# Seven block products with their sums taken in PSUM by later matmuls, in place of sums on VectorE

## The chip, the cores and the metric

One core of a Trainium2 chip runs the whole program. The time is that of the device, in microseconds (us). Before: 1896.96 us, the median of three executions (1893.1 to 1897.03). A difference below 0.2% (3.8 us) can't be told from none.

## The reference, cut to what matters

Two layers of a diffusion backbone over 384 tokens (128 of a prompt, 256 of a sample), all in fp32. Each layer projects the normalised tokens h, runs three attention mixers with 16 jobs in all (8 latent heads "mla", 4 grouped-query jobs "gqa", 4 differential heads "diff"), weighs the three outputs with sigmoid gates and ends in 16 experts:

```
z = h @ p['w_in']                      # among its columns g_mla, g_gqa, g_diff, and dq, dk, dv
merged = (sigmoid(g_mla) * (o_mla @ w_br_mla) + sigmoid(g_gqa) * (o_gqa @ w_br_gqa)
          + sigmoid(g_diff) * (o_diff @ w_br_diff))
x = x + gate1 * (merged @ w_out)       # then norm, router, top-k, experts, residual
```

The gate columns, and dq, dk, dv for the sample's tokens, are matrix products of a 2x2 block form. The kernel computes each by seven block products instead of eight (the scheme of Strassen and Winograd), with A and B cut in four:

```
M1 = a11 b11   M2 = a12 b21   M5 = s1 t1   M6 = s2 t2   M7 = s3 t3   M3 = s4 b22   M4 = a22 t4
C11 = M1 + M2          C12 = (M1 + M6) + M5 + M3
C21 = (M1 + M6) + M7 + M4          C22 = (M1 + M6) + M7 + M5
```

C11 and C12 are the halves of `first`, C21 and C22 those of `second` (C21 is columns 0 to 191 of it).

## The kernel before, in words

Every engine has its program written out by hand, with semaphores between them. TensorE is the engine that is always busy; work of VectorE, ScalarE and GpSimd is laid beside it.

**The jobs.** A layer's attention runs as jobs i = 0 to 15. For job i TensorE issues `scores(i)`, `prep(i+1)` (transposes of the next queries and keys), `values(i-1)` (the product "pv" of the job before, only behind odd jobs for mla), then the list `FILL[i]`, which keeps it busy while the softmax runs, and `turn_probs(i)`. ScalarE runs in the order prep(i+1), the exponentials of job i (`exps`, L999), the copy of pv(i-1) out of PSUM (`values`, L1022, L1026, L1030), then its part of FILL[i]. VectorE runs maxima, prep(i+1) (L1343 to L1350), `normalise` (L1361, L1370, L1365), then its part of FILL[i]. Each engine takes its own list strictly in order.

**The blocks.** A block is seven products ("gate" of branch b and unit u, or "two" of half f and q), each of four matmuls with 192 columns; the trace has eight records for each product. They are issued in `product` (L1989) and `two` (L2013). Blocks stand in FILL[5], [6], [7] (gate 0), FILL[8], [9] (two blocks each, behind two projections "c2" of L1951, which ScalarE copies out in L1043), FILL[12] to [15] (gate 1, then two "br1" products of L2041, and in 13 to 15 one "square"), and, behind the jobs, four blocks of gate 2: its first product FILL[16] comes before pv(15), the others are in LAST_GATES. That is 15 blocks in a layer, 30 in all. FILL[7] also has ("adat", 2): two transposes, whose result VectorE takes in L1280.

**The sums.** Before, the order of a block is M5, M1, M2, M6, M3, M7, M4, each product in a bank of its own. ScalarE copies M5 and M1 into PM5 and PM1 (L1053). VectorE does seven additions: L1415 (M2 + PM1), L1417 and L1418 (M6 + PM1 into PU2, + PM5 into PM1), L1421 (M3), L1423 and L1424 (M7), L1426 (M4). Then ScalarE takes the tanh of the pair (L1057). The tanh lets VectorE do the branch's L1393 and L1395.

**The banks.** PSUM has 8 banks. The scores use 0 to 3. `user_banks` gives every product, pv, c2, branch and square ("user") a bank: of 4 to 7, or of 6 and 7 alone for the last two of a fill and outside fills, the one whose last use is oldest. `BEFORE` names the user that held the bank last, and `user_bank` (L1787) makes TensorE wait until ScalarE or VectorE has read that one. Banks 4 and 5 are lent by prep and turn_probs (`borrow`, L2049). Behind the last gate block VectorE copies WB2 (L1572), for which the matmuls of L2325 wait.

Of the kernel before, what the change touches and what calls it, by code (L numbers as in the profile page):

```python
# [18 lines left out]
ALU = mybir.AluOpType  # L19
# [123 lines left out]
M5, M1, M2, M6, M3, M7, M4 = PRODUCTS  # L143
# [5 lines left out]
FILL[7].insert(2, ("adat", 2))  # L149
# [8 lines left out]
FILL[NJ].append(("gate", 2, 0, M5))  # L158
# [45 lines left out]
def by_dve(user):  # L204

    return user[0] in BY_DVE or user[0] in ("gate", "two") and user[3] not in (M5, M1)
# [17 lines left out]

def user_banks():
# [12 lines left out]
    return bank, before  # L238
# [5 lines left out]
BLOCKS = [u for u in USERS if u[0] in ("gate", "two") and u[3] == M5]  # L244


def block_before(user):

    n = BLOCKS.index(user[:3] + (M5,))
    return BLOCKS[n - 1][:3] if n else None  # L250

# [171 lines left out]
DVE_LINKS = 139  # L423
# [3 lines left out]
def backbone(nc, a):  # L427
    ctx = ExitStack()
    with ctx:
# [155 lines left out]

        def held(g, e, c):

            first = c * GE * CAP + e * CAP
            return XG[:, first:first + XW]
# [71 lines left out]
        def _(sp):  # L661
# [8 lines left out]
                     11: [(rows_out, 32), (user_dve, evacuated(USER_AT["gate", 2, 3, M4]))], 12: merged, 13: merged,  # L670
                     14: [(user_mm, USER_AT["out", 0, 1] + 1)], 15: gated, 16: normed,
                     17: jobs_done + [(user_dve, evacuated(USER_AT["gate", 2, 3, M4]))]}
# [50 lines left out]
        def _(pool):  # L723
# [93 lines left out]
            for l in range(DEPTH):  # L817
# [61 lines left out]
                pool.wait_ge(user_dve.s, user_dve.at(l, evacuated(USER_AT["two", 1, 1, M4])))  # L879
# [49 lines left out]
        def _(act):  # L929
# [106 lines left out]
            def fill(l, key):  # L1036
# [9 lines left out]
                elif kind in ("gate", "two"):  # L1046
                    b, u, m = key[1:]
                    if m in (M5, M1):
                        before = block_before(key)
                        if before:  # L1050
                            free = USER_AT[before + ((M7,) if m == M5 else (M3,))]
                            act.wait_ge(user_dve.s, user_dve.at(l, evacuated(free)))
                        user(l, key, lambda ps: nc.scalar.copy(PM5 if m == M5 else PM1, ps[:, 0:HALF]))  # L1053
                    if kind == "gate" and m == M4:
                        pair = (MG[:, 2 * u:2 * u + 2], SG1, SG2[:, 2 * u:2 * u + 2])[b]
                        act.wait_ge(user_dve.s, user_dve.at(l, evacuated(USER_AT[key])))
# [150 lines left out]
        def _(dve):  # L1207
# [190 lines left out]
            def product(l, key):  # L1398


                b, u, m = key[1:]
                n = USER_AT[key]
                if m in (M5, M1):
                    return
                dve.wait_ge(user_mm.s, user_mm.at(l, n + 1))
                ps = PS[:, BANK[n], 0:HALF]
                if key[0] == "two":
                    c = 768 * b + TOK * u
                    first, second = ZD[:, 1, c:c + TOK], ZD[:, 2, c:c + TOK]
                else:  # L1410
                    first, second = ((MG[:, 2 * u], MG[:, 2 * u + 1]), (SG1[:, 0], SG1[:, 1]),
                                     (SG2[:, 2 * u], SG2[:, 2 * u + 1]))[b]
                if m == M2:
                    dve.wait_ge(user_act.s, user_act.at(l, evacuated(USER_AT[key[0], b, u, M1])))
                    ins = nc.vector.tensor_tensor(first[:, 0:HALF], ps, PM1, ALU.add)  # L1415
                elif m == M6:
                    link(nc.vector.tensor_tensor(PU2, ps, PM1, ALU.add), l)  # L1417
                    ins = nc.vector.tensor_tensor(PM1, PU2, PM5, ALU.add)  # L1418
                elif m == M3:
                    dve.wait_ge(user_dve.s, user_dve.at(l, evacuated(USER_AT[key[0], b, u, M6])))  # L1420
                    ins = nc.vector.tensor_tensor(first[:, HALF:TOK], ps, PM1, ALU.add)  # L1421
                elif m == M7:
                    link(nc.vector.tensor_tensor(PU2, ps, PU2, ALU.add), l)  # L1423
                    ins = nc.vector.tensor_tensor(second[:, HALF:TOK], PU2, PM5, ALU.add)  # L1424
                else:
                    ins = nc.vector.tensor_tensor(second[:, 0:HALF], ps, PU2, ALU.add)  # L1426
                ins.then_inc(user_dve.s, 1)
# [51 lines left out]
            for l in range(DEPTH):  # L1479
# [40 lines left out]
                for i in range(NJ + 1):  # L1520
# [17 lines left out]
                    for key in FILL[i]:  # L1538
                        if key[0] in ("gate", "two"):
                            product(l, key)  # L1540
                            if i in (14, 15) and key[3] == M4:
# [18 lines left out]
                for key in LAST_GATES:  # L1560
# [4 lines left out]
                    if key[2:] == (0, M4):  # L1565
                        inverse(l, 3).then_inc(recd_ok.s, 1)
                    if key[2:] == (1, M4):
# [203 lines left out]
        def _(pe):  # L1771
# [203 lines left out]
            def product(l, key):  # L1975
# [12 lines left out]
                for k in range(4):  # L1988
                    ins = pe.matmul(ps[:, 0:HALF], lhs[:, k], rhs[:, k], start=k == 0, stop=k == 3)  # L1989
# [6 lines left out]
            def two(l, key):  # L1996
# [14 lines left out]
                done = {M1: units[0:2], M3: units[2:4]}.get(m) if q else None  # L2011
                for k in range(4):
                    ins = pe.matmul(ps[:, 0:HALF], lhs[:, k], rhs[k], start=k == 0, stop=k == 3)  # L2013
# [543 lines left out]
```

## Time and profile before

| | us |
|---|---|
| median of three executions | 1896.96 |
| the profiled execution, its own time | 1892.48 |
| its span, first to last instruction | 1890.7 |
| TensorE busy | 1758.8 (93% of the span) |
| VectorE busy | 672.1 (36%) |
| ScalarE busy | 332.8 (18%) |
| GpSimd busy | 320.1 (17%) |

The mean granted TensorE clock is 0.987 of full speed. The jobs with blocks of the first layer lie at 157 to 375 us, its last gates at 375 to 416, its experts at 513 to 945. The second layer repeats this 935.7 us later. In the rows PE is TensorE, DVE VectorE, ACT ScalarE, POOL GpSimd. A row of a timeline gives the start, the length, and in square brackets how long the engine was idle before it and who ended that; x8 is eight instructions merged in one row.

### The profile page before, as it was taken

The numbers are of one execution on the slowest core, as the hardware profiler recorded it, in microseconds if no ns is written. First come the engines' busy times: TensorE is split into PE (matmuls) and PEld (weight loads), VectorE is DVE, ScalarE is ACT, GpSimd is POOL, SyncE is SP. The second block draws the span as 40 slices with busy tenths as digits, with TensorE's granted clock in tenths as the row PEclk, the third lists the DMA queues.
The fourth block names the chain that finished last, engine by engine and source line by source line (L and its number), as shares of the span: only waits on it lengthen the run. The fifth ranks groups of instructions, "written<-read, shape, count | busy, mean of one in ns | idle before, by whom it ended". The sixth has DMA issues, their size and how long they took to land.

```text
span 1890.7 us, 21687 instructions
## 1 busy us (share of the span) xinstructions
PE 1758.8 (93%) x8638; PEld 977.0 (52%) x8638; DVE 672.1 (36%) x1385; ACT 332.8 (18%) x818; POOL 320.1 (17%) x349
## 2 busy tenths in 40 slices
PE   7999999999999998889799999999998999897886
PEld 5557877784533323233255587788844333332322
DVE  2235547742412212121123554567423221211212
ACT  3332213220201001000032322232112010100101
POOL 0234654320000000000002446523200000000000
PEclk9999999999899999999999999999999999999999
DMA  9245231249499999999961632322548999999997
GB/s 372 107 180 218 95 119 49 88 184 418 180 429 429 429 429 429 429 430 428 427 236 53 270 146 79 123 79 101 225 191 349 430 428 429 429 428 430 429 428 296
DMA packets 58227, 541.15 MB, mean 286 GB/s; under 512 B 7001, under 2 KB 7433, under 8 KB 14353
## 3 DMA queue, kind: packets, MB, share of 16 engines
q1 hardware_dynamic: 56592, 535.65, 68.5%
q0 software_dynamic: 1536, 4.13, 0.6%
q8 instruction: 70, 1.15, 0.2%
q14 instruction: 29, 0.23, 0.0%
HBM read 536.54 MB, written 3.21 MB: 285 GB/s over the span
## 4 chain that ended last, share of the span: by engine, by line
PE 78%; DMA 12%; DVE 4%; SPq 3%; ACT 2%; issue 1%; DVEq 0%; ACTq 0%
PE banks L2437 25%; PE banks L1989 10%; DMA arena<-in_w_exp 7%; PE banks L1951 7%; PE banks L2041 7%; PE banks L1798 4%; PE banks L2356 4%; PE banks L2013 4%; SPq L695 3%; DMA ring<-in_w_exp 3%; PE banks L2516 2%; PE banks L1906 2%; PE banks L2214 2%; PE banks L2155 1%; PE banks L2412 1%; DMA ring<-in_w_att 1%
## 5 line engine op out<-in xcount | busy, mean ns | idle before, releaser
L2437 PE MATMUL banks<-arena 128*64 128x512 f32 x1680 | 382.1, 599 | 28.8 <-DMA arena<-in_w_exp 17.0
L2437 PE MATMUL banks<-ring,arena 128*64 128x512 f32 x1392 | 313.0, 595 | 23.4 <-DMA ring<-in_w_exp 13.3
L2437 PEld LDWEIGHTS banks<-arena 128*64 128x64 f32 x1680 | 117.5, 138 | 271.8 <-issue 220.0
L2437 PEld LDWEIGHTS banks<-ring,arena 128*64 128x64 f32 x1392 | 97.0, 137 | 222.0 <-issue 178.0
L1734 DVE TENSOR_TENSOR arena<-banks,arena 32x512 f32<-32x512 f32 (+1 forms) x128 | 87.9, 687 | 265.7 <-PE banks L2437 264.4
L1951 PE MATMUL banks<-ring,arena 128*128 128x384 f32 (+1 forms) x416 | 132.8, 478 | 0.7 <-ACT arena L949 0.7
L1798 PE MATMUL banks<-arena 128*128 128x128 f32 (+3 forms) x734 | 107.9, 283 | 26.5 <-DVE arena L1719 18.9
L1798 PEld LDWEIGHTS banks<-arena 128*128 128x128 f32 (+3 forms) x734 | 84.2, 142 | 87.6 <-issue 37.6
L2041 PE MATMUL banks<-arena,ring 128*128 128x384 f32 x384 | 126.8, 488 | 0.0
L1189 ACT ACTIVATE arena<-banks 128x512 f32<-128x512 f32 x32 | 19.1, 597 | 508.5 <-PE banks L2437 508.5
L1951 PEld LDWEIGHTS banks<-ring,arena 128*128 128x128 f32 x416 | 78.2, 190 | 50.9 <-issue 1.5
L823 POOL COPY arena<-arena 128x32 f32<-128x32 f32 x4 | 0.8, 210 | 598.2 <-ACT arena L1087 597.9
L1989 PE MATMUL banks<-ring 128*128 128x192 f32 x544 | 96.9, 328 | 0.8 <-DVE arena L1395 0.8
L2041 PEld LDWEIGHTS banks<-arena,ring 128*128 128x128 f32 x384 | 72.2, 190 | 48.8 <-issue 1.5
L1719 DVE TENSOR_TENSOR arena<-arena,banks 128x512 f32<-128x512 f32 x32 | 22.0, 687 | 209.4 <-PE banks L2437 209.4
L1989 PEld LDWEIGHTS banks<-ring 128*128 128x128 f32 x544 | 89.0, 190 | 2.8 <-DVE arena L1395 1.3
L2356 PE MATMUL banks<-ring,arena 128*128 128x512 f32 x192 | 86.4, 604 | 1.2 <-DVE arena L1395 1.2
L1716 DVE TENSOR_TENSOR arena<-banks,arena 128x512 f32<-128x512 f32 x32 | 22.1, 691 | 171.4 <-ACT arena L1189 171.4
L925 POOL TENSOR_TENSOR arena<-arena 128x1024 f32<-128x1024 f32 x1 | 2.4, 2363 | 442.6 <-DVE arena L1744 442.6
L999 ACT ACTIVATE arena<-banks,arena 128x384 f32<-128x384 f32 x144 | 71.4, 508 | 19.0 <-DVE arena L1335 18.7
L2516 PE MATMUL banks<-arena 128*128 128x512 f32 (+1 forms) x112 | 51.9, 617 | 21.7 <-DVE arena L1734 18.6
L1333 DVE TENSOR_REDUCE arena<-banks 128x1 f32<-128x384 f32 x144 | 58.4, 460 | 28.0 <-PE banks L2155 16.5
(264 smaller groups left out, 2110.8 us busy)
## 6 DMA issues: line engine op xcount, KB each, us to landing
arena<-in_w_exp SPq DMA_DIRECT2D x69, 2048.0 KB, 30.7
ring<-in_w_exp SPq DMA_DIRECT2D x69, 2048.0 KB, 29.6
ring<-in_w_att SPq DMA_DIRECT2D x80, 1024.0 KB, 7.0
arena<-in_w_exp SPq DMA_DIRECT2D x72, 1024.0 KB, 26.7
ring<-in_w_exp SPq DMA_DIRECT2D x36, 1024.0 KB, 13.4
ring<-in_w_att SPq DMA_DIRECT2D x26, 768.0 KB, 7.9
arena<-in_w_att SPq DMA_DIRECT2D x12, 1024.0 KB, 11.6
ring<-in_w_att SPq DMA_DIRECT2D x8, 672.0 KB, 8.7
```

The source lines that it names most:

```text
L695: sp.dma_start(span(group), a["w_exp"][l, c0:c1].rearrange("(p n) -> p n", p=P))\
L999: ins = nc.scalar.activation(PB[:, b, lo:hi], PS[:, 2 * m + bank, c:c + hi - lo], ACT.Exp, scale=SCALE[kind], bias=NB[:, b, r:r + 1], accu ...
L1333: ins = nc.vector.reduce_max(MX[:, b, r:r + 1], PS[:, 2 * m + bank, c:c + w], AX)
L1734: ins = nc.vector.tensor_tensor(y[32 * e:32 * e + hi - lo, BF * h:BF * h + BF], PS[64 * h + lo:64 * h + hi, 5], G2[64 * h + lo:64 * h + hi ...
L1798: return pe.transpose(out, src, IDT[0:rows, 0:rows])
L1951: ins = pe.matmul(ps[:, 0:width], hT[:, k, P * t:P * t + P], slots[n][:, c0:c0 + width], start=k == 0, stop=k == KC - 1)
L1989: ins = pe.matmul(ps[:, 0:HALF], lhs[:, k], rhs[:, k], start=k == 0, stop=k == 3)
L2013: ins = pe.matmul(ps[:, 0:HALF], lhs[:, k], rhs[k], start=k == 0, stop=k == 3)
L2041: ins = pe.matmul(ps[:, 0:TOK], w[:, k, P * (c % 4):P * (c % 4) + P], o[:, k], start=k == 0, stop=k == 3)
L2356: ins = pe.matmul(ps, MG[:, k, P * t:P * t + P], slots[n][:, c0:c0 + BF], start=k == 0, stop=k == KC - 1)
L2437: ins = pe.matmul(PS[64 * h:64 * h + 64, bank], lhs(k), slots[i][:, c0:c0 + BF], start=k == 0, stop=k == KC - 1)
L2516: ins = pe.matmul(combine_bank(g, n)[:, c:c1], w, YS[0 if t else 1][:, BF * h + c:BF * h + c1], start=True, stop=True)
```

## The change

The order of a block becomes M1, M5, M6, M2, M7, M3, M4. M6, M7 and M4 are added by TensorE to the bank in which M1 stands (start=False), and M3 to the bank of M5. Only M1, M5 and M2 open a bank. ScalarE copies the bank out after M1 (PM1), M5 (PM5), M6 (now PU2 = M1 + M6) and M4 (straight into C21). VectorE keeps three additions: M2 + PM1, M7's bank + PM5, M3's bank + PU2. So M6 waits for the copy of M1, M7 for that of M6, M3 for that of M5, and M4 for VectorE's reading of M7's bank.

A block in a fill has the banks 6 (M1 and its sums) and 7 (M5) and M2 in 4 or 5; the first of two blocks in a fill has 4 and 5, and M2 in 6 or 7. Behind the jobs they alternate between 6, 7 and 0, 1, with M2 and the last square in 2 or 3. ("adat", 2) moves from the third place of FILL[7] to the first. Worked through, `user_banks` gives: adat bank 7, and M5 behind it bank 7; c2's second projection bank 4, and M1 behind it bank 4; pv(5), pv(11) to pv(15) bank 7, and M5 behind each of them bank 7; the square of FILL[15] bank 6, and M1 of gate 2 behind it bank 6.

```diff
-M5, M1, M2, M6, M3, M7, M4 = PRODUCTS
+M1, M5, M6, M2, M7, M3, M4 = PRODUCTS
+OPENS, CLOSES = (M1, M5, M2), (M2, M3, M4)
...
-FILL[7].insert(2, ("adat", 2))
+FILL[7].insert(0, ("adat", 2))
...
-FILL[NJ].append(("gate", 2, 0, M5))
+FILL[NJ].append(("gate", 2, 0, M1))
...
-    return user[0] in BY_DVE or user[0] in ("gate", "two") and user[3] not in (M5, M1)
+    return user[0] in BY_DVE or user[0] in ("gate", "two") and user[3] in (M2, M7, M3)
...
-    bank, before, latest, holder = [], [], {6: -2, 7: -1}, {}
+    bank, before, latest, holder = [], [], {6: -2, 7: -1, 2: -4, 3: -3}, {}
+    after = [u for u in BLOCKS if u not in fill_of]
...
-        b = min((4, 5, 6, 7) if left > 2 else (6, 7), key=lambda x: latest[x])
+        block = user[:3] + (M1,)
+        if block in BLOCKS:
+            if left:
+                behind = sum(u in BLOCKS for u in FILL[i][FILL[i].index(block) + 1:])
+                sums, rest = ((6, 7), (4, 5))[::1 if behind % 2 == 0 else -1]
+            else:
+                sums, rest = ((6, 7), (0, 1))[after.index(block) % 2], (2, 3)
+            if user[3] == M2:
+                b = min(rest, key=lambda x: latest[x])
+            else:
+                b = sums[user[3] in (M5, M3)]
+        elif user[0] == "square" and not left:
+            b = min((2, 3), key=lambda x: latest[x])
+        else:
+            b = min((4, 5, 6, 7) if left > 2 else (6, 7), key=lambda x: latest[x])
...
-                elif kind in ("gate", "two"):
+                elif kind in ("gate", "two") and not by_dve(key):
                     b, u, m = key[1:]
-                    if m in (M5, M1):
+                    if m == M4:
+                        user(l, key, lambda ps: nc.scalar.copy(halves(key)[1][:, 0:HALF], ps[:, 0:HALF]))
+                    else:
                         before = block_before(key)
                         if before:
-                            free = USER_AT[before + ((M7,) if m == M5 else (M3,))]
+                            free = USER_AT[before + ({M1: M2, M5: M7, M6: M3}[m],)]
                             act.wait_ge(user_dve.s, user_dve.at(l, evacuated(free)))
-                        user(l, key, lambda ps: nc.scalar.copy(PM5 if m == M5 else PM1, ps[:, 0:HALF]))
+                        kept = {M1: PM1, M5: PM5, M6: PU2}[m]
+                        user(l, key, lambda ps: nc.scalar.copy(kept, ps[:, 0:HALF]))
...
-                if m == M2:
-                    dve.wait_ge(user_act.s, user_act.at(l, evacuated(USER_AT[key[0], b, u, M1])))
-                    ins = nc.vector.tensor_tensor(first[:, 0:HALF], ps, PM1, ALU.add)
-                elif m == M6:
-                    link(nc.vector.tensor_tensor(PU2, ps, PM1, ALU.add), l)
-                    ins = nc.vector.tensor_tensor(PM1, PU2, PM5, ALU.add)
-                elif m == M3:
-                    dve.wait_ge(user_dve.s, user_dve.at(l, evacuated(USER_AT[key[0], b, u, M6])))
-                    ins = nc.vector.tensor_tensor(first[:, HALF:TOK], ps, PM1, ALU.add)
-                elif m == M7:
-                    link(nc.vector.tensor_tensor(PU2, ps, PU2, ALU.add), l)
-                    ins = nc.vector.tensor_tensor(second[:, HALF:TOK], PU2, PM5, ALU.add)
-                else:
-                    ins = nc.vector.tensor_tensor(second[:, 0:HALF], ps, PU2, ALU.add)
-                ins.then_inc(user_dve.s, 1)
+                first, second = halves(key)
+                out, kept, of = {M2: (first[:, 0:HALF], PM1, M1), M7: (second[:, HALF:TOK], PM5, M5),
+                                 M3: (first[:, HALF:TOK], PU2, M6)}[m]
+                dve.wait_ge(user_act.s, user_act.at(l, evacuated(USER_AT[key[:3] + (of,)])))
+                nc.vector.tensor_tensor(out, ps, kept, ALU.add).then_inc(user_dve.s, 1)
...
-                    ins = pe.matmul(ps[:, 0:HALF], lhs[:, k], rhs[:, k], start=k == 0, stop=k == 3)
+                    ins = pe.matmul(ps[:, 0:HALF], lhs[:, k], rhs[:, k], start=k == 0 and m in OPENS, stop=k == 3 and m in CLOSES,
+                                    skip_group_check=True)
```

Left out: the same edit of the matmul in `two`, waits on M4's addition that now name M3's or M4's copy, `inverse` (L1455) that moves from behind M4 to behind M3, and the release of c2's weights, which moves from M1 to M6.

## Rows read from the trace of the kernel before

**Rows 1.** Busy time by stretch: us, then busy us (instructions) of each engine, clock, DMA.
```profile
157.00:416.00 259.00, 256.62 (x1456) 212.88 (x1454) 153.80 (x324) 70.64 (x201) 116.95 (x111) 1.00 0.28 105
1093.00:1352.00 259.00, 256.61 (x1455) 213.14 (x1454) 152.82 (x322) 70.77 (x201) 116.14 (x109) 1.00 0.28 105
513.00:945.00 432.00, 385.83 (x1776) 139.69 (x1774) 87.90 (x147) 30.19 (x62) 0.00 (x0) 0.98 1.01 429
480.00:513.00 33.00, 30.06 (x144) 19.21 (x144) 18.94 (x61) 10.15 (x22) 0.00 (x0) 0.79 0.40 162
```
**Rows 2.** Line 1053 alone: shortest, median and longest duration in ns.
```profile
L1053 ACT COPY arena<-banks x60: 299/318/366, 159.7 to 1344.2; 128x192 f32<-128x192 f32 x60
```
**Rows 3.** Timeline of job 5, a bank that TensorE waits for.
```profile
158.54 0.69 DVE L1344 COPY arena<-banks 64x512 f32<-64x512 f32 x1
...
159.29 0.43 PE L1989 MATMUL banks<-arena,ring 128*128 128x192 f32 x1 [0.18 <-DVE arena L1344]
```
**Rows 4.** Timeline of job 7, first layer.
```profile
184.02 1.47 PE L1989 MATMUL banks<-ring 128*128 128x192 f32 x8
...
185.32 1.46 PE L1989 MATMUL banks<-arena,ring 128*128 128x192 f32 x8
...
187.63 0.44 PE L1798 MATMUL banks<-arena 128*128 128x128 f32 x2 [0.84 <-DVE arena L1350]
...
187.90 1.47 PE L1989 MATMUL banks<-arena,ring 128*128 128x192 f32 x8
188.79 0.24 DVE L1280 TENSOR_TENSOR arena<-banks,arena 128x8 f32<-128x8 f32 x2
```
**Rows 5.** Timelines of jobs 12, 13, 15 and the last gates: second product, pv's copy.
```profile
302.13 1.46 PE L1989 MATMUL banks<-arena,ring 128*128 128x192 f32 x8
...
302.60 0.50 ACT L1026 COPY arena<-banks 128x384 f32<-128x384 f32 x1
...
321.30 2.12 PE L1989 MATMUL banks<-arena,ring 128*128 128x192 f32 x12
...
322.14 0.50 ACT L1030 COPY arena<-banks 128x384 f32<-128x384 f32 x1
...
360.22 2.60 PE L1989 MATMUL banks<-arena,ring 128*128 128x192 f32 x15
...
361.78 0.50 ACT L1030 COPY arena<-banks 128x384 f32<-128x384 f32 x1
...
378.08 1.46 PE L1989 MATMUL banks<-arena,ring 128*128 128x192 f32 x8
378.28 0.48 ACT L1030 COPY arena<-banks 128x384 f32<-128x384 f32 x1 [1.15 <-PE banks L2214]
```
**Rows 6.** Timeline of job 8: the first product behind the c2 projections.
```profile
209.54 1.46 PE L2013 MATMUL banks<-ring 128*128 128x192 f32 x8
209.74 0.48 ACT L1043 COPY arena<-banks 128x384 f32<-128x384 f32 x1 [4.68 <-PE banks L1951]
```
**Rows 7.** Timeline at the end of job 15.
```profile
373.97 1.13 DVE L1395 TENSOR_TENSOR arena<-arena 128x384 f32<-128x384 f32 x1
...
375.02 0.54 DVE L1449 TENSOR_SCALAR arena<-banks 128x384 f32<-128x384 f32 x1
375.15 1.57 PE L1989 MATMUL banks<-ring 128*128 128x192 f32 x8 [0.40 <-DVE arena L1395]
```
**Rows 8.** Timeline behind the last gate block.
```profile
415.38 0.61 PE L2325 MATMUL banks<-arena 2*128 2x16 f32 x4 [0.52 <-DVE arena L1572]
```
**Rows 9.** Busy time by stretch around a long and a shorter idle time of TensorE.
```profile
612.00:615.60 3.60, 0.50 (x5) 0.03 (x1) 2.76 (x4) 0.00 (x0) 0.00 (x0) 1.00 1.01 432
615.60:619.00 3.40, 3.40 (x6) 2.10 (x7) 0.69 (x1) 0.00 (x0) 0.00 (x0) 0.50 0.98 419
...
1372.00:1375.40 3.40, 2.16 (x6) 0.87 (x5) 1.49 (x3) 0.00 (x0) 0.00 (x0) 1.00 1.02 431
```
**Rows 10.** TensorE's waits behind VectorE: us in total, times, longest us.
```profile
PE banks L2516 <- DVE arena L1734: 18.6, 6, 3.1
```

More of the change, by code:

```diff
@@ L222, in evacuated @@
     return sum(by_dve(u) == dve for u in USERS[:n + 1])
+BLOCKS = [u for u in USERS if u[0] in ("gate", "two") and u[3] == M1]
 def user_banks():
     fill_of = {u: (i, len(FILL[i]) - k) for i in range(NJ) for k, u in enumerate(FILL[i])}
-    bank, before, latest, holder = [], [], {6: -2, 7: -1}, {}
+    bank, before, latest, holder = [], [], {6: -2, 7: -1, 2: -4, 3: -3}, {}
+    after = [u for u in BLOCKS if u not in fill_of]
     for n, user in enumerate(USERS):
@@ L241 @@
 BANK, BEFORE = user_banks()
-BLOCKS = [u for u in USERS if u[0] in ("gate", "two") and u[3] == M5]
 def block_before(user):
-    n = BLOCKS.index(user[:3] + (M5,))
+    n = BLOCKS.index(user[:3] + (M1,))
     return BLOCKS[n - 1][:3] if n else None
@@ L420 @@
 RAW_DVE, PROMPT_DVE = (1, 3, 4), (2,) + tuple(range(5, 4 + KC))
-DVE_LINKS = 139
+DVE_LINKS = 109
 POOL_LINKS = 58
@@ L584, in span, with halves @@
             return at(first, 2 * SLOT)
+        def halves(key):
+            kind, b, u = key[:3]
+            if kind == "two":
+                c = 768 * b + TOK * u
+                return ZD[:, 1, c:c + TOK], ZD[:, 2, c:c + TOK]
+            return ((MG[:, 2 * u], MG[:, 2 * u + 1]), (SG1[:, 0], SG1[:, 1]), (SG2[:, 2 * u], SG2[:, 2 * u + 1]))[b]
         def held(g, e, c):
@@ L878, in _ @@
                 pool.wait_ge(user_act.s, user_act.at(l, evacuated(USER_AT["c2", 7])))
-                pool.wait_ge(user_dve.s, user_dve.at(l, evacuated(USER_AT["two", 1, 1, M4])))
+                pool.wait_ge(user_act.s, user_act.at(l, evacuated(USER_AT["two", 1, 1, M4])))
+                pool.wait_ge(user_dve.s, user_dve.at(l, evacuated(USER_AT["two", 1, 1, M3])))
                 for t in range(2):
@@ L1398, in product @@
             def product(l, key):
[L1401 removed]
+                m = key[3]
+                if not by_dve(key):
+                    return
                 n = USER_AT[key]
[L1403 to L1404 removed]
                 dve.wait_ge(user_mm.s, user_mm.at(l, n + 1))
                 ps = PS[:, BANK[n], 0:HALF]
[L1407 to L1427 removed]
+                first, second = halves(key)
[3 more added lines that the diff above has]
+                nc.vector.tensor_tensor(out, ps, kept, ALU.add).then_inc(user_dve.s, 1)
             def token_sums_first(l):
@@ L1540, in _ @@
                             product(l, key)
-                            if i in (14, 15) and key[3] == M4:
+                            if i in (14, 15) and key[3] == M3:
                                 inverse(l, i - 14)
@@ L1564, in _ @@
                     product(l, key)
-                    if key[2:] == (0, M4):
+                    if key[2:] == (0, M3):
                         inverse(l, 3).then_inc(recd_ok.s, 1)
-                    if key[2:] == (1, M4):
+                    if key[2:] == (1, M3):
                         dve.wait_ge(rootd_ok.s, rootd_ok.at(l, 1))
@@ L2010, in two @@
                             M4: (a22, t4)}[m]
-                done = {M1: units[0:2], M3: units[2:4]}.get(m) if q else None
+                done = {M6: units[0:2], M3: units[2:4]}.get(m) if q else None
                 for k in range(4):
-                    ins = pe.matmul(ps[:, 0:HALF], lhs[:, k], rhs[k], start=k == 0, stop=k == 3)
+                    ins = pe.matmul(ps[:, 0:HALF], lhs[:, k], rhs[k], start=k == 0 and m in OPENS, stop=k == 3 and m in CLOSES,
+                                    skip_group_check=True)
                     if k == 0:
```

7 lines of the change are left out of this document (4 added, 3 removed).

## The prediction, made before the changed kernel ran

> **What bounds the kernel now.** First the busy time by stretch. In the 259.0 us of the first layer that hold every block, TensorE is busy for 256.62, at full clock, and in the second layer for 256.61 [rows 1]. The reader is to see that 2.4 us a layer is all that TensorE idles there: no relief of VectorE can bring more than about 4.8 us in both layers together, while any new wait of TensorE is paid in full. Next VectorE in the same row. It is busy for 153.80 of the same 259 us, so it bounds nothing [rows 1]. Last the timelines, for two questions at each block: which user held the bank before, and when was it read? They are what decides here, since each engine takes its list in order.
>
> **Units of the working.** Products follow each other by 185.32 - 184.02 = 1.30 us [rows 4]. Where TensorE waits for a reader, the restart can be priced: L1344 ends at 158.54 + 0.69 = 159.23, the waiting matmul begins at 159.29 and is 0.10 longer than the normal 0.33 of a matmul with 192 columns [rows 3]. So work goes on **0.16 us after the end of the read**. And since a matmul's row reaches 0.16 beyond the start of the next (eight rows last 1.46, not 1.30), a printed idle time of x is a loss of x + 0.16.
>
> **What the change removes and adds.** Of VectorE's seven additions four go, 120 in all. ScalarE gets two more copies a block of 0.32 us [rows 2], 60 in all, about 19 us. TensorE has the same matmuls. Adding to a bank is what three of four matmuls in each product do already, in rows of the same length; I take nothing for it, and know of no row for a gain or a loss. The four additions and the copies are hidden behind TensorE. If the cover of the copies were gone, it would cost M6 and M7 up to 0.32 each.
>
> **Waits inside a block.** M6 adds to M1's bank, and one product (1.30 us) lies between. A copy starts about 0.4 us behind a product's last matmul, lasts 0.32 and is seen 0.16 later: 0.9 of the 1.46 us to the first matmul of M6. The same holds for M7 behind M6's copy and for M4 behind VectorE's addition. So they cost nothing while ScalarE is free. In the jobs it first does the exponentials and pv's copy. In job 12 that copy ends at 303.10 [rows 5]; M1's follows and frees M6 at about 303.6, while M6's turn, behind an M5 that starts at 303.26 (below), is 304.56. I count nothing more. A square root on ScalarE between two copies of gate (2, 1) is counted at nothing too; some tenths at most.
>
> **The banks across users** are where it costs. Per layer:
> - *pv and M5.* M5, now second, takes bank 7, which held the pv product issued just before the block. Its copy stands on ScalarE behind the exponentials. Before, the fourth or fifth product had that bank. Job 12: the second product starts at 302.13; the copy ends at 302.60 + 0.50, so M5 starts at 303.26: 1.13 us lost. Job 13: 322.14 + 0.50 + 0.16 = 322.80 against 321.30, 1.50; job 14 repeats it, 1.50. Job 15, with no prep before it: 362.44 against 360.22, 2.22. The last gates: 378.28 + 0.48 + 0.16 = 378.92 against 378.08, 0.84 [rows 5]. Job 6 has the same pattern with 0.28. Sum **7.47**.
> - *adat in job 7.* Moved to the front it takes bank 7, and M5 takes bank 7 behind it. VectorE reads adat only after its key copies and `normalise`: 188.79 + 0.24 [rows 4], so M5 starts at 189.19, with adat and M1 done and six products to go: end at 189.19 + 7.80 = 196.99. Before, five products were to go at 187.90 (a wait of 0.84 for L1350 included, which disappears): end at 194.40 [rows 4]. **2.59**.
> - *c2 and M1.* M1 takes bank 4, from which c2's second projection is just being copied: 209.74 + 0.48 + 0.16 = 210.38 against 209.54 [rows 6], 0.84. Jobs 8 and 9: **1.68**.
> - *The square.* M1 of the last gates waits for L1449 on bank 6, ending at 375.56, where it waited for L1395, ending at 375.10 [rows 7]: **0.46**.
> - *Gains.* The wait for L1344 goes, 0.18 + 0.16 + 0.10 = 0.44 with the restart [rows 3]; one for a slow L1418 in job 6, 0.2; and L1572 no longer stands behind an addition of the last product: 0.52 + 0.16 = 0.68 [rows 8]. **-1.32**.
>
> 7.47 + 2.59 + 1.68 + 0.46 - 1.32 = 10.88 us a layer, **21.8 us** in both; the second layer's rows repeat the first's. SP's queue keeps its transfers, and the waits it gets are not later ones. GpSimd's block sums are awaited by M5, now one product later.
>
> **TensorE's clock.** It stood at full speed in both stretches with the blocks [rows 1]. Job 7's new wait leaves TensorE idle for some 3.4 us at a time. An idle time of 3.10 us before 615.6 was followed by 3.4 us at half the clock, that is 1.2 GHz instead of 2.4, in which 1.7 us of work are lost; one of 1.24 us, within 1372.0 to 1375.4, was not [rows 9]. The trace has six idle times of 3.10 us, all for L1734 [rows 10]; by the clock column four were followed by such a spell. Bounds for the clock: nothing, or four spells (job 7 and job 15 in both layers), 6.8 us. I take the two of job 7, the rows nearest to them being those of 3.10: 3.4 us.
>
> Sum: 21.8 + 3.4 = **25.2 us**. The profiled execution has a span of 1890.7 and a time of 1892.48, so it would go to 1915.9 and 1917.7. It lies 4.5 us below the median of the executions shown, a difference between executions that no step of mine touches. Forecast: 1896.96 + 25.2 = **1922.1 us**.
>
> **Rivals.**
> 1. *The clock falls in every long wait.* By the Trainium skill ("TensorE: Matmul & The Clock Gate", section "A second HAM failure mode: psum-queue depth-cycling") short idle times between groups of matmuls that cycle through banks are enough to make the clock go down and up. The waits of jobs 7 and 12 to 15 would each bring a spell of 1.7 us: 10 x 1.7 = 17 us in place of 3.4, 1935.8 us. Against it: the idle time of 1.24 us [rows 9], as long as those of jobs 13 and 14 would be printed, left the clock up. Chance 0.07. By that rule the sum is 38.8 us, by the rows 25.2.
> 2. *The experts' transfers take the loss up.* From 513 to 945 the DMA engines move 429 GB/s all the time [rows 1]. If that stream kept its times, TensorE would come late to the experts and find the weights there. Against it: from 480 to 513 they move only 162 [rows 1], since all places are full until TensorE uses one, so the stream starts with TensorE and shifts with it. Wholly taken up, the time is 1897; by half, 1908 to 1910. Chance 0.08, half of it for no measurable difference.
> 3. *Faster: ScalarE comes in time.* With VectorE's queue shorter, maxima and exponentials could end sooner, so that pv's copy is over before the second product. The point at which this decides is in job 12: the copy has to end by 301.97 and not at 303.10 [rows 5], and in job 15 2.2 us earlier. Then adat has to be read early as well. What remains are the gains, 2 x 1.32 = 2.6 us, and at most the 4.8 us of idle time: 1892 to 1894. Against it: in those jobs the exponentials follow maxima that VectorE does before any of the additions that go. Chance 0.03.
> 4. *Fewer of the waits appear.* If pv's copies were awaited but M5's place were mostly covered, only adat, c2 and the square would be left: 2 x (4.73 - 1.32) = 6.8 us, 1903.8. Nothing in the profile says so. Chance 0.05.
>
> **How the numbers follow.** The forecast has 0.77. Its own range is 1916 to 1927: the sum without a clock spell is 1918.7, with four 1925.5, and executions differ by some us. The range for 8 in 10 goes down to 1909, to the case of half the loss taken up, and up to 1931, towards the clock. Within 0.2% (about what a measurement of this kernel can tell from no change): 0.04, from rival 2. Faster: 0.03. Slower: 0.93.
>
> **What would show it.** In the profile after: idle time of L1989 put down to ScalarE's L1026 and L1030 in jobs 12 to 15, 0.9 to 2.0 us each as printed; one of some 3.4 us in job 7, put down to VectorE's L1280; 0.6 us of L2013 behind ScalarE's L1043, four times; TensorE's busy time in the blocks' stretch unchanged but the stretch some 11 to 13 us longer; the experts' stretch as long as before. The prediction is wrong if TensorE's idle time before L1989 and L2013 together stays under 10 us in both layers, or if the experts' stretch gets shorter.

## The result: slower by 1.35%, and where the time went

| | before | after |
|---|---|---|
| median of five executions | 1894.88 us | 1918.68 us |
| the profiled execution, its span | 1890.7 us | 1919.6 us |

The ratio is 1.0135, with a 95% interval of 1.0122 to 1.0147: 23.1 to 27.9 us on 1894.88. The two medians differ by 23.8 us. The forecast was 1922.1 us, the range 1909 to 1931.

The trace has 8638 matmul records of TensorE in both kernels, in the same order but for the two transposes of adat in each layer, so the start of the n-th record of one can be subtracted from that of the other. That shift grows by 1.45 us ahead of the first block, by 13.57 us in the first layer's stretch with blocks, by 13.42 us in the second's, and by 0.43 us in all the rest, experts included: 28.9 us. The 27.0 us of the two stretches are the change; what lies ahead of the blocks differs from one execution to the next (in the kernels below the shift there is between -0.7 and +2.1 us). The profiled execution of after, at 1921.46 us, was the slowest of its five, which is one reason why 27.0 is more than the 23.8 us between the medians.

Busy time of the kernel after, by stretch, in the columns of [rows 1]:

```profile
157.00:427.00 270.00, 258.88 (x1434) 212.95 (x1433) 126.09 (x263) 79.27 (x229) 117.02 (x113) 0.99 0.27 100
1105.00:1375.00 270.00, 258.88 (x1433) 212.44 (x1432) 122.50 (x263) 79.52 (x230) 119.25 (x114) 0.99 0.27 100
525.00:957.00 432.00, 384.53 (x1788) 140.72 (x1789) 89.14 (x152) 32.11 (x67) 0.00 (x0) 0.99 1.01 429
```

Against [rows 1] TensorE now idles 11.1 us in each stretch with blocks instead of 2.4, and the clock is at 0.99 instead of 1.00. VectorE is busy for 126 us instead of 154, and TensorE got nothing of it. The idle time explains 8.7 of the 13.5 us of a stretch; most of the rest is the clock, of which more below, since matmuls at half speed count as busy. The experts' stretch keeps its 429 GB/s. Who is waited for (engine and line of the waiting instruction, engine and line that ended the wait, us in total, times, longest):

```profile
PE banks L2002 <- ACT arena L1055: 10.0, 8, 2.0
...
PE banks L2002 <- DVE arena L1309: 6.8, 2, 3.4
...
PE banks L2027 <- ACT arena L1068: 2.3, 4, 0.6
...
PE banks L2002 <- ACT arena L1051: 1.7, 2, 0.9
...
PE banks L2002 <- DVE arena L1462: 0.6, 2, 0.3
```

L2002 and L2027 are the block products (before: L1989, L2013). L1055 and L1051 are ScalarE's copies of pv, L1309 is VectorE's reading of adat, L1068 the copy of c2, L1462 the square's. Each of these is a bank's reader that was not awaited before: eighteen waits, 21.4 us as printed, plus a restart each.

The groups of the additions and copies (busy us, mean ns): three additions a block are left on VectorE, and ScalarE has four copies:

```profile
L1440 DVE TENSOR_TENSOR arena<-banks,arena 128x192 f32<-128x192 f32 x90 | 32.2, 358 | 198.2 <-PE banks L2002 121.0 <-PE banks L2027 77.3
...
L1081 ACT COPY arena<-banks 128x192 f32<-128x192 f32 x90 | 28.4, 318 | 83.3 <-PE banks L2002 56.4 <-PE banks L2027 26.7
...
L1074 ACT COPY arena<-banks 128x192 f32<-128x192 f32 x30 | 9.6, 320 | 144.1 <-PE banks L2002 105.5 <-PE banks L2027 38.6
```

Jobs 7 and 15 in the timeline of after, where [rows 4] and [rows 5] show the kernel before:

```profile
185.31 1.47 PE L2002 MATMUL banks<-arena,ring 128*128 128x192 f32 x8
...
190.15 4.55 PE L2002 MATMUL banks<-ring 128*128 128x192 f32 x16 [3.38 <-DVE arena L1309]
...
195.83 1.46 PE L2002 MATMUL banks<-ring 128*128 128x192 f32 x8
...
197.13 1.46 PE L2002 MATMUL banks<-arena 128*128 128x192 f32 x8
...
372.92 0.50 ACT L1055 COPY arena<-banks 128x384 f32<-128x384 f32 x1
...
373.47 4.20 PE L2002 MATMUL banks<-ring,arena 128*128 128x192 f32 x16 [1.96 <-ACT arena L1055]
```

The products at 195.83 and 197.13 are M7 and M3, added to banks that ScalarE has read: 1.30 us from one to the next, as in [rows 4]. But behind the two waits something is longer. Sixteen matmul records of two products should last 2.87 us behind a wait (that is what they last behind the 1.23 us in job 13). Here they last 4.55 and 4.20. The cause stands in the clock column of the windows:

```profile
190.50:193.90 3.40, 3.40 (x13) 3.40 (x12) 0.40 (x2) 0.32 (x1) 0.00 (x0) 0.50 0.00 0
374.80:378.20 3.40, 3.40 (x13) 3.40 (x12) 0.23 (x1) 0.64 (x2) 2.88 (x3) 0.51 0.00 0
```

TensorE's granted clock is half, 1.2 GHz instead of 2.4, for 3.4 us behind both waits. The second layer shows the same twice (from 1139.4 and 1323.7 us), which makes four spells in this execution. No trace shows how many the other four executions had.

### The profile page after: what moved, and what is told of

It reads as the page before. It is cut to its first block, busy times and chain, and to the rows that moved or that the text cites. A ratio compares the mean times of both kernels' runs of the same rounds, so it can differ in the third digit from the quotient of the medians.

```text
span 1919.6 us, 21699 instructions
## 1 busy us (share of the span) xinstructions
PE 1767.0 (92%) x8638; PEld 980.6 (51%) x8638; DVE 613.0 (32%) x1265; ACT 352.3 (18%) x878; POOL 317.7 (17%) x349
## 4 chain that ended last, share of the span: by engine, by line
PE 76%; DMA 12%; DVE 5%; ACT 3%; SPq 3%; issue 1%; DVEq 0%; ACTq 0%
PE banks L2452 25%; PE banks L2002 10%; DMA arena<-in_w_exp 7%; PE banks L1964 7%; PE banks L2056 7%; PE banks L2027 4%; PE banks L1811 4%; PE banks L2371 4%; SPq L719 3%; DMA ring<-in_w_exp 3%; PE banks L2531 2%; PE banks L1919 2%; PE banks L2170 1%; DMA ring<-in_w_att 1%; PE banks L2427 1%; PE banks L2297 1%
## 5 line engine op out<-in xcount | busy, mean ns | idle before, releaser
L2002 PE MATMUL banks<-ring 128*128 128x192 f32 x544 | 102.0, 335 | 12.1 <-DVE arena L1309 6.8
L2002 PEld LDWEIGHTS banks<-ring 128*128 128x128 f32 x544 | 92.7, 195 | 15.4 <-DVE arena L1309 7.3
L1440 DVE TENSOR_TENSOR arena<-banks,arena 128x192 f32<-128x192 f32 x90 | 32.2, 358 | 198.2 <-PE banks L2002 121.0
L1024 ACT ACTIVATE arena<-banks,arena 128x384 f32<-128x384 f32 x144 | 71.5, 509 | 18.3 <-DVE arena L1364 18.0
```

Of the source, the lines that this page charges most:

```text
L1024: ins = nc.scalar.activation(PB[:, b, lo:hi], PS[:, 2 * m + bank, c:c + hi - lo], ACT.Exp, scale=SCALE[kind], bias=NB[:, b, r:r + 1], accu ...
```

## The experiments

All edits are made to the changed kernel. Each kernel has line numbers of its own. This table gives the growth of the shift against the kernel before, in the first layer, in us. A job's column goes from its scores to the next job's; that of job 15 takes in M1 of the last gates and pv(15). The second layer agrees within 0.2 us.

```
                 job 5  job 6  job 7  job 8  9 to 12  job 13  job 14  job 15  last gates   sum
after            -0.45  +0.06  +4.26  +0.83   +1.96   +1.50   +1.50   +3.80     +0.11     13.57
e1_adat          -0.45  +0.07  -1.04  +0.84   +1.96   +1.50   +1.50   +2.12     +0.11      6.61
e2_pv            -0.45  -0.21  +4.26  +0.83   +0.89   +0.96   +0.96   +1.58     -0.63      8.19
e3_c2            -0.44  +0.06  +4.27   0.00   +1.14   +1.50   +1.50   +2.12     +0.11     10.26
e4_all           -0.44  -0.21  -1.04   0.00   +0.04   +0.96   +0.96   +1.57     -0.64      1.20
e5_best          -0.45  -0.21  -1.04   0.00   +0.05   +0.96   +0.96   +1.01     -0.63      0.65
e9_ahead         -0.45  -0.21  -1.04   0.00    0.00    0.00    0.00   -0.06     -0.64     -2.40
e10_after_exps   -0.45  -0.21  -1.04   0.00    0.00   +0.04   +0.04   +0.09     -0.64     -2.16
e7_dve           -0.45  -0.21  -1.04  +0.06   +0.06    0.00    0.00   +0.24     -0.50     -1.84
e8_near          +0.77  +0.52  +1.28  +1.46   +1.46    0.00    0.00   +0.03     +1.83      7.36
e6_long          -0.45  +0.06  +4.27  +0.83   +1.96   +2.23   +1.91   +2.11     +0.11     13.04
```

### Each wait undone by itself: e1_adat, e2_pv, e3_c2

**e1_adat** puts adat back to its third place in FILL[7]:

```diff
-FILL[7].insert(0, ("adat", 2))
+FILL[7].insert(2, ("adat", 2))
```

> The changed kernel with adat back in the third place of FILL[7]. Theory (waits on a bank whose last user is read late): job 7 loses neither the wait of M5 for L1280 (3.65 us as a loss) nor the spell of half clock behind it (1.7), in both layers: 10.7 us less than the changed kernel, ratio to before about 1.008, and no half-clock spell in job 7. Rival A (the moved waits are harmless and the chain of additions inside the blocks costs the time, some 0.8 us a block): within 2 us of the changed kernel, 1.0125 or more.

Measured: 1905.69 us, ratio 1.006 (1.0041 to 1.0079). Job 7 loses nothing any more; it gains 1.04 us, since the wait for L1350 that the kernel before had there is gone as well and no spell of the clock follows. More came back than its own stretch: in job 15 the idle time is still 1.96 us, but this time no spell follows it.

```profile
366.90:371.90 5.00, 5.00 (x31) 5.00 (x32) 1.86 (x5) 1.32 (x4) 3.17 (x3) 1.00 0.01 3
```

These are the five microseconds behind that wait, with the clock at 1.00 where after had 0.51. The column of job 15 falls from 3.80 to 2.12, so the spell was a term of its own, 1.68 us.

**e3_c2** gives the first of two blocks in a fill the banks in the other order, so that M1 does not take the one just left by c2:

```diff
-                sums, rest = ((6, 7), (4, 5))[::1 if behind % 2 == 0 else -1]
+                sums, rest = ((6, 7), (4, 5)) if behind % 2 == 0 else ((5, 4), (6, 7))
```

> The changed kernel with banks 5 and 4 exchanged in the first of two blocks of a fill, so that M1 no longer takes the bank of c2's second projection. Theory: four waits of 0.84 us go, 3.4 us less than the changed kernel, ratio about 1.0118, and no idle time of L2027. Rival A: no difference from the changed kernel (1.0135).

Measured: 1914.05 us, ratio 1.0106 (1.0087 to 1.0125). Jobs 8 and 9 stand where they stood before the change. Both layers together give back 3.3 us there. In job 15 no spell follows the idle time here either (+2.12).

**e2_pv** keeps M5 off the bank that pv holds:

```diff
+            if left and i in (6, 12, 13, 14, 15):
+                sums, rest = (6, 5), (7,)
+            elif block == ("gate", 2, 0, M1):
+                sums, rest = (6, 1), (2, 3)
             if user[3] == M2:
```

> The changed kernel with M5 and M3 of jobs 6 and 12 to 15 in bank 5 (in the first block behind the jobs: bank 1) and M2 in bank 7, so that no second product needs the bank of the pv just issued. Theory: 7.47 us of waits a layer go, and the spell in job 15 (1.7): 18.3 us less than the changed kernel, ratio to before about 1.004; M2, the fourth product, finds bank 7 read. Rival A: within 2 us of the changed kernel. Rival B (pv's copy is late for M2 as well, so the wait only moves from M5 to M2): the waits in jobs 13 to 15 shrink, but some idle time before M2 stays, and less than 10 us is won.

Measured: 1911.68 us, ratio 1.009 (1.007 to 1.011). This is 7.0 us less than the changed kernel, less than half of the 18.3 that the first theory claimed. Rival B was right that less than 10 us would be won and that a wait would take the place of the old one, but not about the product: the one that waits is M6, the third, and not M2. The waits of e2_pv in the first layer:

```profile
PE banks L2006 <- DVE arena L1313: 3.4, 1, 3.4
PE banks L2006 <- ACT arena L1085: 2.8, 3, 1.4
```

L1085 is ScalarE's copy *inside* the block. The wait for pv's copy is gone and M6's wait for M1's copy has come forward in jobs 13, 14 and 15.

### All three together: e4_all and e5_best

> The three edits together, the sums still in PSUM. Theory: what is left of the change is its gains, 1.3 us a layer, and job 7's old wait for L1350 (1.0 us) that is gone as well: about 5 us below the kernel before, ratio 0.9973 (0.996 to 0.9985). Rival A (additions in PSUM, or M6, M7 and M4 tied to one bank, cost time of their own): slower than before, above 1.002. No difference from before (0.999 to 1.001) would say that the banks were the whole loss and VectorE's relief is worth nothing.

Measured: 1896.11 us over ten executions, ratio 1.0009 (0.9998 to 1.002). The ratio alone would fit the last sentence of the expectation, that the banks were the whole loss and nothing was gained. The trace shows otherwise: the gains of jobs 5 to 7 and of the last gates are there, 2.3 us a layer, and a new wait of 3.5 us a layer takes them away again. The timeline of that wait in job 13 (start, length):

```profile
321.56 0.50 ACT L1059 COPY arena<-banks 128x384 f32<-128x384 f32 x1
...
322.09 0.52 ACT L1063 ACTIVATE arena<-arena 128x384 f32<-128x384 f32 x1
...
322.52 0.52 ACT L1085 COPY arena<-banks 128x192 f32<-128x192 f32 x2
...
322.87 1.57 PE L2006 MATMUL banks<-ring,arena 128*128 128x192 f32 x8 [0.69 <-ACT arena L1085]
```

M1 was done at 319.42 + 1.47 = 320.89, yet its copy stands behind the exponentials, pv's copy (L1059) and the square of pv (L1063), and starts at 322.52. M6 adds to M1's bank and has to wait for it. In job 12 the pv before it is of a gqa head and no square follows: 0.04 us for jobs 9 to 12 together. The kernel after had M5 wait longer still, for pv's copy, so M6 was late anyway and this wait had cover.

**e5_best** gives the first of the last gates `sums = (0, 1)`, away from the bank of the square. With it the pairs of the three other last gates change places too: 6 and 7, then 0 and 1, then 6 and 7.

> As e4_all, but the first of the last gates has its sums in banks 0 and 1 instead of 6 and 1, so that its M1 waits neither for the square nor for the second br1 addition. M1 stays behind pv in jobs 12 to 15. Theory: only that wait goes, 0.3 us and a restart in each layer, 0.9 in both: 1895.2 us, with M6's waits for M1's copy as in e4_all (5.6 us printed). So e9_ahead's gain is 0.9 from here and the rest from M1's place. Rival: what M1 doesn't wait for, a matmul of the same place waits for next (pv needs the probabilities' copies): 1896.1.

Measured: 1893.41 us, ratio 0.9998 (0.9987 to 1.0008). In the table only job 15 moves, by 0.56 us a layer: the wait of 0.30 us printed, 0.16 for the overlap of the rows and 0.10 for the restart. The medians of e4_all and e5_best lie further apart (2.7 us) than the 1.1 us that the blocks explain, and differ in stretches that the edit does not touch.

### The order on ScalarE: e9_ahead and e10_after_exps

Both start from e5_best. In jobs 12 to 15 M1 is issued ahead of pv. In e9_ahead ScalarE copies it between the exponentials of the two maps; in e10_after_exps behind both, but still ahead of pv's copy. The last of these pieces is in e9_ahead alone; left out are the same step in the lists of TensorE and ScalarE:

```diff
+EARLY = (12, 13, 14, 15, NJ)
...
+    _k = int(_i in EARLY)
+    USERS += FILL[_i][:_k]
     if _i >= 1 and values_of(_i - 1):
         USERS.append(("pv", _i - 1))
-    if _i < NJ:
-        USERS += FILL[_i]
+    USERS += FILL[_i][_k:]
...
                     ins.then_inc(exp_ok.s, 1)
+                    if m == 0 and j in EARLY:
+                        fill(l, FILL[j][0])
```

> The repairs of adat, c2 and pv's place, bank 0 instead of 6 for the first of the last gates, and in jobs 12 to 15 M1 issued ahead of pv, with ScalarE copying it between the exponentials of the two maps instead of behind them, behind pv's copy and behind the square. Theory: with the other waits repaired, the one left is M6's for M1's copy (+0.96, +0.96 and +1.68 us in jobs 13, 14, 15 against the kernel before, in each layer), so it goes, 7.2 us in both layers, and the square's wait with its restart 0.9: 1896.1 - 8.1 = 1888.0 us, 0.997 of before; no row of L2006 behind L1085. Rival: ScalarE's copy between the maps holds up the second map and the normalisation, and the time moves to the transposes at the end of the fill: 1896, 1.001.

> As e9_ahead, but ScalarE copies M1 behind both maps' exponentials (still ahead of pv's copy and the square). Theory (what matters is where the copy stands on ScalarE): jobs 13 and 14 lose nothing (copy over at 321.84, M6's turn 322.02), job 15 waits 363.11 + 0.26 + 0.16 - 362.87 = 0.66 us, twice: 1889.3 us. Rival (the square and pv's copy are not what held M1's copy): as e4_all less 0.9, 1895.2.

Measured: e9_ahead 1889.09 us, ratio 0.9973 (0.9964 to 0.9982); e10_after_exps 1888.0 us, ratio 0.997 (0.996 to 0.9981). **Both beat both kernels.** Job 15 of e9_ahead in the timeline, with M1's copy between the maps and M6 not waiting:

```profile
360.12 2.76 PE L2006 MATMUL banks<-ring,arena 128*128 128x192 f32 x16
360.13 0.20 ACT L1026 ACTIVATION_READ_ACCUMULATOR arena<-banks,arena 128x1 f32 x1
360.22 0.32 ACT L1085 COPY arena<-banks 128x192 f32<-128x192 f32 x1
...
360.42 0.61 ACT L1026 ACTIVATE arena<-banks,arena 128x384 f32<-128x384 f32 x1
...
373.42 1.27 POOL L840 TENSOR_TENSOR arena<-ring,arena 128x512 f32<-128x512 f32 x1
...
373.86 1.24 DVE L1428 TENSOR_TENSOR arena<-arena 128x384 f32<-128x384 f32 x1
...
376.32 0.46 PE L2230 MATMUL banks<-arena 128*128 128x128 f32 x2 [0.37 <-DVE arena L1574]
```

The same job of e10_after_exps:

```profile
359.51 0.34 ACT L1083 COPY arena<-banks 128x192 f32<-128x192 f32 x1
...
359.91 1.57 PE L2004 MATMUL banks<-ring,arena 128*128 128x192 f32 x8 [0.49 <-ACT arena L1083]
...
370.83 1.58 POOL L840 TENSOR_TENSOR arena<-ring,arena 128x512 f32<-128x512 f32 x1
...
372.46 0.56 DVE L1426 TENSOR_TENSOR arena<-arena 128x384 f32<-128x384 f32 x1
```

The expected wait of 0.66 us is there (0.49 printed, 0.75 with the overlap and the restart), but it costs only 0.15 us against e9_ahead by the end of the job. The last rows of e9_ahead say why: there pv's matmuls wait 0.37 us for VectorE's L1574, which stands behind the branch's last addition, L1428. In e9_ahead that addition runs beside one of GpSimd and takes 1.24 us. In e10_after_exps GpSimd is done at 372.41, the addition takes 0.56 us (its line there is L1426), and pv doesn't wait. In both it starts 0.6 us ahead of M1 of the last gates, so what went away is not VectorE's lateness against TensorE but the addition's neighbour; the second layer shows the same two durations, 1.23 and 0.56. That wait in e9_ahead is also why the blocks give back 2 x 3.60 = 7.2 us from e4_all to e9_ahead and not the 8.1 expected. TensorE's busy time in the stretches of [rows 1], e9_ahead:

```profile
157.00:416.00 259.00, 258.19 (x1462) 214.25 (x1461) 126.31 (x266) 79.90 (x231) 117.40 (x113) 1.00 0.28 105
1093.00:1352.00 259.00, 258.20 (x1457) 213.94 (x1457) 124.77 (x264) 78.79 (x228) 114.81 (x109) 1.00 0.30 109
```

So 4.8 us in both layers (2 x 2.40) is what the blocks give. TensorE still idles 0.8 us in each stretch, against 2.4 before [rows 1]; the gain is larger than the difference since each wait that goes also takes its overlap and its restart with it.

### Is it VectorE's relief? e7_dve

```diff
                 nc.vector.tensor_tensor(out, ps, kept, ALU.add).then_inc(user_dve.s, 1)
+                for _ in range({M2: 1, M7: 1, M3: 2}[m]):
+                    link(nc.vector.tensor_tensor(SPARE, CST[:, 0:160], CST[:, 160:320], ALU.add), l)
```

> As e9_ahead, plus four dummy additions of 160 columns on VectorE in each of the 30 blocks (120 in all, as many as the change took away; chained behind the three that are left). Theory (taking work from VectorE is worth nothing here, since TensorE waits for it nowhere in a block): within 1 us of e9_ahead, VectorE's busy time some 30 us longer. Rival (the gains of e9_ahead come from VectorE's relief): some us slower, back towards the kernel before, 1893.7.

Measured: 1889.79 us, ratio 0.998 (0.9972 to 0.9989), 0.7 us from e9_ahead. The group of the dummy additions, and the stretch of the first layer:

```profile
L1447 DVE TENSOR_TENSOR arena<-arena 128x160 f32<-128x160 f32 x120 | 60.3, 503 | 1.1
```

```profile
157.00:416.00 259.00, 257.90 (x1461) 214.22 (x1460) 151.20 (x322) 80.01 (x231) 117.02 (x111) 1.00 0.29 106
```

With 60.3 us more on VectorE (I had reckoned with 30), which puts it at 151.20 in this stretch, near the 153.80 of [rows 1], most of the gain stays: 1.84 of the 2.40 us of this layer. So it does not come from VectorE's lower load. But the dummies do not stand where the additions stood. Two parts of the gain, 0.85 us a layer, do come from additions that left VectorE's queue: in job 6 of the kernel before TensorE had waited behind a slow L1418 (0.21), and in the last gates WB2's copy (L1572, [rows 8]) stood behind the addition of the last product (0.64):

```profile
414.89 0.36 DVE L1426 TENSOR_TENSOR arena<-banks,arena 128x192 f32<-128x192 f32 x1 [0.55 <-PE banks L1989]
415.17 0.15 DVE L1572 COPY arena<-banks 2x16 f32<-2x16 f32 x1
```

The larger part, 1.49 us in jobs 5 and 7, is two waits for bank 4, which prep had lent (VectorE's key copies L1344 and L1350), and they went with the banks' new places. Whether the kernel before would win it too, with its sums on VectorE and other banks for those two users, was not tested.

### What a read in the middle costs: e8_near

```diff
-M1, M5, M6, M2, M7, M3, M4 = PRODUCTS
+M1, M6, M5, M2, M7, M3, M4 = PRODUCTS
```

> As e9_ahead, but M6 directly behind M1 (order M1, M6, M5, M2, M7, M3, M4), no product between them. In the 10 blocks where pv lies between the two nothing changes; in the other 20 M6 comes 1.30 us earlier while ScalarE's copy needs 0.4 + 0.32 + 0.16 us behind M1's last matmul. Theory (a later product can be added to a read bank for nothing when one product of 1.30 us lies between, and costs the copy's whole way when none does): 0.73 us a block, 14.6 us, and some 4 us more in jobs 5 to 7, where M1's copy stands behind the exponentials: about 1907 us. Rival (the read costs nothing even then): 1888.

Measured: 1908.04 us, ratio 1.0073 (1.0053 to 1.0093). The waits:

```profile
PE banks L2006 <- ACT arena L1085: 9.4, 14, 1.3
...
PE banks L2031 <- ACT arena L1085: 3.7, 8, 0.5
```

Jobs 8 and 9 have two blocks each and the shift grows by 1.46 us in each: 0.73 us a block, as worked out. So a bank that is read between two products costs nothing with one product of 1.30 us between, and 0.73 us with none. In job 7 it is 2.32 us against e9_ahead: 1.54 for M6's wait for M1's copy, which stands behind exponentials there, and 0.78 for a wait of M5 for VectorE's reading of adat, whose bank 7 it takes in this order.

### How long an idle time lowers the clock: e6_long

```diff
+                if j == 12:
+                    nc.scalar.copy(SPARE[:, 0:768], CST[:, 0:768])
+                if j == 13:
+                    nc.scalar.copy(SPARE[:, 768:1152], CST[:, 0:384])
                 act.wait_ge(user_mm.s, user_mm.at(l, n + 1))
```

> The changed kernel with one more copy on ScalarE ahead of pv's copy in job 13 (768 columns, some 0.8 us) and in job 14 (384 columns, some 0.4 us), so that TensorE's wait there is printed as about 2.0 and 1.6 us instead of 1.24. Theory (the clock falls after long idle times only): a spell of 3.4 us at 1.2 GHz behind the one of 2.0 in each layer, and none or some behind 1.6; time 1918.7 + 2.4 + 3.4 = 1924.5 us, with spells in both jobs 1927.9. Rival (what lowers the clock in job 15 is something else of that job, not the length of the idle time): no spell in jobs 13 and 14, 1921.1.

Measured: 1919.26 us, ratio 1.0136 (1.0123 to 1.015); nearer to the rival's number. The wait in job 13 of the first layer in the timeline, then the clock behind it in the windows:

```profile
331.78 2.87 PE L2007 MATMUL banks<-ring,arena 128*128 128x192 f32 x16 [1.96 <-ACT arena L1060]
```

```profile
331.60:335.00 3.40, 3.22 (x20) 3.22 (x21) 1.01 (x3) 1.44 (x5) 2.18 (x2) 1.00 0.00 0
```

No spell here, nor behind 1.64 us in job 14, nor, this time, behind 1.95 us in job 15, in either layer. So neither theory holds as I had put it: the length of the idle time does not decide alone at 1.95 us, and it is no property of job 15 either.

## Why the prediction was right, and which steps were not

**Right, with their terms** (predicted and measured, per layer): the waits for pv in jobs 12 to 14, 1.13, 1.50 and 1.50 us, measured as 1.13, 1.50 and 1.50; job 15, 2.22, measured as 2.22 (2.12 in the column of e1_adat, in which the 0.10 gained at the square is counted); c2, 0.84 a job, measured 0.83; the wait for L1344 that goes, 0.44 and 0.45; L1572, 0.68 and 0.63; adat, 2.59, and 4.26 - 1.68 for the spell = 2.58 (the column of the second layer has 4.09, since there the spell began 0.31 us before TensorE went on, and half of that was not lost). The rule behind them, that work goes on 0.16 us after the end of the read, 0.10 of it the restart, held throughout. The sentence behind it in the prediction, that a printed idle time of x is a loss of x + 0.16, forgets that restart: 1.96 printed was a loss of 2.22, 1.23 one of 1.50. In the sum only the gain at L1572 was reckoned with it. The experts took nothing up (rival 2), ScalarE did not come early (rival 3), and no expected wait was missing (rival 4).

**The clock term was too small for the profiled execution.** "I take the two of job 7": four spells came, which was the upper bound of that step, 6.6 us instead of 3.4. Behind 3.4 us of idle time a spell followed in every case (job 7 of after, e2_pv, e3_c2 and e6_long, both layers). Behind 1.95 to 1.96 us in job 15 it followed in both layers of after, and in neither layer of e1_adat, e3_c2 and e6_long. Behind 1.23 or 1.24 us it never did. So whether a typical execution of after has two spells or four, these traces do not decide. Rival 1 is wrong for jobs 12 to 14. The trace of the kernel before already had a row nearer to job 15 than the two that the prediction took, the experts' wait of 1.94 us and the clock behind it:

```profile
703.15 7.07 PE L2437 MATMUL banks<-arena 128*64 128x512 f32 x24 [1.94 <-DMA arena<-in_w_exp]
```

```profile
704.30:707.80 3.50, 3.50 (x10) 0.98 (x8) 0.00 (x0) 0.00 (x0) 0.00 (x0) 0.51 1.04 442
```

Behind 1.93 us at 792.4 the same trace has another spell, and behind 1.96 us at 814.3 none. By the Trainium skill ("TensorE: Matmul & The Clock Gate", section "A second HAM failure mode: psum-queue depth-cycling") short idle times between groups of matmuls that cycle through banks, when they are frequent, are enough. In the blocks the traces agree for 3.38 us and, sometimes, for 1.96, and not for 1.24. But from 480 to 513 us of the kernel before the mean clock is 0.79 [rows 1] with no idle time of TensorE above 0.94 us, so the length of one idle time is not all there is to it; no run here looks into that stretch.

**The square's step failed.** "M1 of the last gates waits for L1449 on bank 6 ... 0.46": the wait is there but TensorE comes out of it 0.10 us earlier than before. The timeline of the kernel before and then that of after:

```profile
373.42 1.27 POOL L814 TENSOR_TENSOR arena<-ring,arena 128x512 f32<-128x512 f32 x1
...
373.97 1.13 DVE L1395 TENSOR_TENSOR arena<-arena 128x384 f32<-128x384 f32 x1
```

```profile
387.23 1.58 POOL L838 TENSOR_TENSOR arena<-ring,arena 128x512 f32<-128x512 f32 x1
...
389.00 0.56 DVE L1424 TENSOR_TENSOR arena<-arena 128x384 f32<-128x384 f32 x1
...
389.48 0.55 DVE L1462 TENSOR_SCALAR arena<-banks 128x384 f32<-128x384 f32 x1
...
390.08 1.57 PE L2002 MATMUL banks<-arena,ring 128*128 128x192 f32 x8 [0.30 <-DVE arena L1462]
```

The branch's last addition took 1.13 us while GpSimd worked beside it, and 0.56 once GpSimd was done at 388.81. It started 0.55 us behind GpSimd's last addition in the kernel before and 1.77 us behind it in the one after. The step carried the duration over from before, where that neighbour ran beside it. By the Trainium skill ("GPSIMD Engine Reference", section "1. Specifications") the two engines share their SBUF interfaces and contend when a VectorE instruction has two SBUF inputs. The traces agree, 1.13 us against 0.56.

**"They cost nothing while ScalarE is free"** was true of the kernel after, but for a reason that I had written down in one number only: M6's turn "is 304.56", behind an M5 that waits. I had not followed it to its consequence, that the same chain on ScalarE is worth 3.5 us a layer once M5's wait is mended. e2_pv found it, and e9_ahead shows that it was the place on ScalarE: moving one copy ahead of pv's copy and the square took the sum from 0.65 to -2.40 us.

The sum was 25.2 us. Measured in the blocks' stretches of the profiled executions it is 27.0: 3.2 more for the clock, 1.1 less for the square, and 0.2 less over the small terms, most of it in the last gates' wait for pv (0.73 instead of 0.84). So a part of the close agreement is luck: two errors of opposite sign cancel in part, and the clock term may differ between executions.

## What to carry to other kernels

Sums in PSUM cost nothing by themselves here, with one product between a read and the next addition; what cost most of the 27 us was which bank the product behind a slow reader took, and the rest was the clock that fell behind the longest of these waits. Follow for each bank who reads it last and what stands ahead of that reader on its engine, and do so again after each repair, since the next reader in that queue is the next wait. A lower load on an engine that TensorE does not wait for gives next to nothing (four dummy additions a block cost 0.6 us a layer), while one 0.36 us addition that left the place ahead of an awaited copy gave 0.6, and moving one 0.3 us copy ahead in ScalarE's queue gave 3. And a duration carried over from the trace of before holds only while the same neighbours run beside it.

## What the runs showed of the hardware beyond the forecast

- An idle time of TensorE of 1.95 to 1.96 us was followed by 3.4 us at half clock in two of eight cases at one and the same place in the program, with the same block products before and behind. What decides it is open; the length of this idle time alone does not.
- Such a spell cost 1.68 us where it lay wholly within work (job 15 of after against e1_adat, both layers). Where it began before TensorE went on it cost less: behind the same wait of 3.38 us in job 7 of the second layer, a start 0.31, 0.16, 0.08 and 0 us ahead of the first matmul (after, e2_pv, e3_c2, e6_long) went with a growth of 4.09, 4.17, 4.20 and 4.25 us.
- A VectorE addition of 128x384 with both inputs in SBUF took between 0.56 us, with GpSimd done, and 1.40 us beside it (e10_after_exps); in the kernel before the longest was 1.13. A dummy addition of 128x160 took 503 ns in the mean, more than the 358 ns of the 128x192 ones that read a bank.
- An addition by TensorE to a bank that ScalarE had read in the meantime lasted as long as into a fresh one: 1.30 us from product to product in both kernels.
